# Value projection of the second layer by seven block products in place of eight

## The reference

```python
        else:
            o = layer // 2
            qc, kc, vc = jnp.split(h @ odd_w_in[o], 3, axis=-1)
            mix = stick_breaking_attention(qc, kc, vc) @ odd_w_out[o]
        h = layer_norm(DEEPNORM_ALPHA * h + mix, ln_mix_g[layer], ln_mix_b[layer])
        ffn = swiglu(h, ffn_w1[layer], ffn_w3[layer], ffn_w2[layer])
```

## Time and profile before

| | |
|---|---|
| median of 3 runs | 1157.35 us (1156.26 to 1157.83) |
| the profiled execution | 1156.23 us, its span 1154.5 us |
| PE busy | 1133.9 us, 98% of the span |
| PEld (weight loads of PE) | 988.1 us, 86% |
| DVE / ACT / POOL busy | 863.0 / 541.4 / 525.2 us |
| granted TensorE clock, mean | 0.998 of full speed |
| the chain that ended last | PE 92%, DVE 5%, ACT 1%, POOL 1% |

### The profile page before, as it was taken

One profiled execution on the slowest core, in us unless ns is written; L12 is line 12 of the kernel. 1 busy time (PEld: TensorE's weight loads), 2 busy tenths in 40 slices (PEclk: granted clock), 3 DMA queues, 4 the chain that ended last, 5 costly groups with the idle time before them and its releaser, 6 DMA issues.

```text
span 1154.5 us, 19191 instructions
## 1 busy us (share of the span) xinstructions
PE 1133.9 (98%) x7461; PEld 988.1 (86%) x7461; DVE 863.0 (75%) x1202; ACT 541.4 (47%) x849; POOL 525.2 (45%) x346
## 2 busy tenths in 40 slices
PE   7999999999999999999999999999999999999997
PEld 6877768899999999888887777777999999998886
DVE  8558652897888888994804787866987888879957
ACT  6335665245444544553335555532545454454540
POOL 6897614356567773010353232203576666760000
PEclk9999999999999999999999999999999999999999
DMA  7623315143333336234243111202433333352341
GB/s 213 186 76 93 109 65 201 39 126 110 110 100 103 108 105 192 72 113 143 86 133 91 56 56 55 67 8 74 130 89 111 110 105 97 100 179 88 96 123 73
DMA packets 160186, 121.00 MB, mean 105 GB/s; under 512 B 19376, under 2 KB 140248, under 8 KB 160096
## 3 DMA queue, kind: packets, MB, share of 16 engines
q1 hardware_dynamic: 160096, 119.77, 34.7%
HBM read 116.32 MB, written 3.43 MB: 104 GB/s over the span
## 4 chain that ended last, share of the span: by engine, by line
PE 92%; DVE 5%; ACT 1%; POOL 1%; issue 1%; SPq 0%; DMA 0%; DVEq 0%; ACTq 0%; POOLq 0%
PE ps L2122 18%; PE ps L2124 17%; PE ps L2123 17%; PE ps L2154 5%; PE ps L2152 5%; PE ps L2153 5%; PE ps L2145 5%; PE ps L2147 5%; PE ps L2146 5%; PE ps L2661 2%; PE ps L2687 2%; PE ps L2672 2%; PE ps L2159 1%; PE ps L2705 1%; PE ps L2384 1%; PE ps L2707 1%
## 5 line engine op out<-in xcount | busy, mean ns | idle before, releaser
L848 POOL TENSOR_TENSOR wlo<-raw,whi 128x1024 fp32r<-128x1024 f32 x75 | 183.2, 2454 | 333.4 <-ACT whi L973 326.4
L2122 PE MATMUL ps<-xhi,whi 128*128 128x256 f32 (+1 forms) x848 | 272.1, 321 | 0.0
L2124 PE MATMUL ps<-xhi,wlo 128*128 128x256 f32 (+1 forms) x848 | 267.0, 315 | 0.0
L2123 PE MATMUL ps<-xlo,whi 128*128 128x256 f32 (+1 forms) x848 | 266.9, 315 | 0.0
L2122 PEld LDWEIGHTS ps<-xhi,whi 128*128 128x128 f32 x848 | 161.7, 191 | 17.6 <-issue 6.4
L927 POOL TENSOR_TENSOR wlo<-raw,whi 128x512 fp32r<-128x512 f32 x114 | 173.2, 1546 | 0.6 <-ACT whi L1235 0.4
L2124 PE MATMUL ps<-thi,wlo 128*128 128x256 f32 x608 | 172.2, 283 | 0.0
L2123 PE MATMUL ps<-tlo,whi 128*128 128x256 f32 x608 | 172.2, 283 | 0.0
L2122 PE MATMUL ps<-thi,whi 128*128 128x256 f32 x608 | 172.2, 283 | 0.0
L2124 PEld LDWEIGHTS ps<-xhi,wlo 128*128 128x128 f32 x848 | 161.8, 191 | 10.4
L2123 PEld LDWEIGHTS ps<-xlo,whi 128*128 128x128 f32 x848 | 161.9, 191 | 8.5
(11 more groups left out here) (293 smaller groups left out, 2355.6 us busy)
## 6 DMA issues: line engine op xcount, KB each, us to landing
raw<-in_ffn_w SPq DMA_DIRECT2D x126, 512.0 KB, 3.9
raw<-in_odd_w_in SPq DMA_DIRECT2D x24, 512.0 KB, 3.7
raw<-in_even_w_in SPq DMA_DIRECT2D x16, 512.0 KB, 4.5
t<-in_ffn_w SPq DMA_DIRECT2D x12, 512.0 KB, 6.4
h<-in_x SPq DMA_DIRECT2D x8, 512.0 KB, 5.0
raw<-in_even_w_out SPq DMA_DIRECT2D x8, 512.0 KB, 3.8
raw<-in_odd_w_out SPq DMA_DIRECT2D x8, 512.0 KB, 3.5
bias<-rel_scratch SPq DMA_DIRECT2D x8, 256.0 KB, 3.5
```

Source lines behind the costliest of these rows:

```text
L848: eng.tensor_tensor(lo, raw_of(b), hi, ALU.subtract).then_inc(w_lo, 1)
L2122: eng.matmul(o_, w_hi_, x_hi_, start=start, stop=False)
L2123: eng.matmul(o_, w_hi_, x_lo_, start=False, stop=False)
L2124: return eng.matmul(o_, w_lo_, x_hi_, start=False, stop=stop)
```

## The change

The token rows, the k values and the columns are each cut in half, x = [[A11, A12], [A21, A22]] and W = [[B11, B12], [B21, B22]], and the four quarters of the result come from seven products of quarter matrices (256 tokens x 512 k x 512 columns), in Winograd's form of Strassen's scheme:

- P1 = A11·B11, P2 = A12·B21, P4 = A22·(B21 − B22 + B12 − B11), P7 = (A11 − A21)·(B22 − B12), P6 = (A21 + A22 − A11)·(B22 − B12 + B11), P5 = (A21 + A22)·(B12 − B11), P3 = (A12 + A11 − A21 − A22)·B22;
- C11 = P1 + P2, C12 = P1 + P6 + P5 + P3, C21 = P1 + P4 + P7 + P6, C22 = P1 + P7 + P6 + P5. In the code P6 is summed onto P7 in the same two banks, so C12 first has P7 subtracted.

Each product is two units of 12 matmuls (two tiles of k, two token tiles, three products): 14 units, 168 matmuls, in the order P1, P2, P4, P7, P6, P5, P3. The first four units go through `overlapped`, now with one part each.

What comes with it:

- Loads: six blocks of 512 KB for P1, P2 and P3, and four more of 512 KB (`load_right_columns`: B12 and B22) straight into `v1` and `v2`, issued by SP after the last load of the output product; eight were there before.
- POOL: eight differences of weights of 128x1024 (`v_sums`). The two for P7 stand ahead of the wait for the last block of the output product, the six others after the lowering of the first block of P1. Then it lowers 14 blocks in place of 8; for four products the block is a difference, not a landed one.
- ACT: keeps the unrounded x of the first two token tiles in `xf` (`keep_x`), copies P1 to `sg` (`keep_first`), rounds 14 blocks of weights and four sums of x (`s_upper`), and copies C11 to `ov`. The four copies of the whole result go.
- DVE: four sums of x (`s_sum` counts them), their four lowerings (`s_lower`), and 14 additions of 128x512 from PSUM (`v_add`).
- PE waits: P7 for the copy of C11 (`ov_out`), for its sum (`s_lowered`); P6, which adds onto P7 in the same banks, for the additions that read P7 (`v_added`); P3 likewise for those that read P5. The first of the products for queries and keys no longer waits for `ov_out`, the scores wait for all 14 additions.

```diff
-    for k in range(KT):
-        row_tiles(owi, k * P, 2 * D, D)
+    V_UNITS = [(p, part) for p in (P1, P2, P4, P7, P6, P5, P3) for part in range(2)]
+    V_END = OV + len(V_UNITS)
+    V_SUMS = [(P7, 0), (P7, 1), (P5, 0), (P6, 0), (P5, 1), (P6, 1), (P4, 0), (P4, 1)]
+    for p, part in V_UNITS:
+        if p in (P1, P2, P3):
+            k0 = 2 * part + (0 if p == P1 else KT // 2)
+            row_tiles(owi, k0 * P, 2 * D + S * (p == P3), S)
+        else:
+            load_of.append(None)
...
+        S_ORDER = (P7, P6, P5, P3)
+        V_BANK = {P1: 0, P2: 0, P4: 2, P7: 0, P6: 0, P5: 4, P3: 4}
+        V_FIRST = (P1, P7, P6, P5)
+        V_ADDS = ([(P4, 0), (P4, 1), (P7, 0), (P7, 1)] + [(P6, t) for t in range(2) for _ in range(3)]
+                  + [(P5, 0), (P5, 1), (P3, 0), (P3, 1)])
...
+                    if OV <= last < V_END and V_UNITS[last - OV][0] != P3:
+                        p, part = V_UNITS[last - OV]
+                        sp_.wait_ge(v_sum, v_sum_upto(P5 if p == P1 else P4, part))
...
+                    if b == out_end(0) - 1:
+                        load_right_columns()
...
+            def load_right_columns():
+                sp_.wait_ge(joint_lo, GS)
+                for part in range(2):
+                    for k0, p in ((0, P5), (KT // 2, P6)):
+                        eng.dma_start(v_store(p, part), tiles_of(owi, (k0 + 2 * part) * P, 2 * D + S, S, 2)).then_inc(
+                            right_landed[part], 16)
...
+            def v_sums(p, part):
...
+                if p == P7:
+                    pool.wait_ge(right_landed[part], 32)
+                    pool.wait_ge(w_used, ordinary(out_first(0) + max(
+                        u for u, unit in enumerate(UNITS[0]) if unit[0] == HALF1) + 1))
+                    o_, a, b_ = t3_, t2_, t1_
+                if p == P5:
+                    pool.wait_ge(*landed(v_block(P1, part)))
+                    pool.wait_ge(v_sum, v_sum_upto(P7, part))
+                    o_, a, b_ = t1_, t1_, upper
+                if p == P6:
+                    pool.wait_ge(v_sum, v_sum_upto(P5, part))
+                    o_, a, b_ = t2_, t2_, t1_
+                if p == P4:
+                    pool.wait_ge(*landed(v_block(P2, part)))
+                    pool.wait_ge(v_sum, v_sum_upto(P6, part))
+                    o_, a, b_ = t4_, lower, t2_
+                eng.tensor_tensor(o_, a, b_, ALU.subtract).then_inc(v_sum, 1)
+
+            v_sums(P7, 0)
+            v_sums(P7, 1)
             pool.wait_ge(w_lo, ordinary(out_end(0)))
-            norm(1, OV)
+            lower_upto(OV + 1)
+            for p, part in V_SUMS[2:]:
+                v_sums(p, part)
+            lower_upto(V_END)
             lower_upto(OQK + LEAD + 4)
...
+                    if summed(b):
+                        act.wait_ge(v_sum, v_sum_upto(*V_UNITS[b - OV]))
...
+                def keep_x(t):
+                    act.wait_ge(x_ready, NT * (n + 1) + t + 1)
+                    eng.copy(xf[:, :, t * P:(t + 1) * P],
+                             psf[:, 2 * t * S:2 * t * S + D].rearrange("p (k n) -> p k n", k=KT)).then_inc(xf_ready, 1)
+
                 for t in range(NT - 1):
                     if n < 3 and t == 2:
                         upper_x(n + 1, 0)
+                        if n == 1:
+                            keep_x(0)
                         upper_x(n + 1, 1)
                     std(t)
                 upper_upto(f + 3)
+                if n == 1:
+                    keep_x(1)
+                    keep_first(0)
                 std(NT - 1)
-                if n < 3:
+                if n == 1:
+                    keep_first(1)
+                    upper_x(2, 2)
+                    upper_upto(f + 4)
+                    upper_x(2, 3)
+                elif n < 3:
                     upper_upto(f + 4)
                     upper_x(n + 1, 2)
                     upper_x(n + 1, 3)
...
+            def keep_first(t):
+                if t == 0:
+                    act.wait_ge(v_first, 1)
+                else:
+                    act.wait_ge(w_used, v_used(P1))
+                eng.copy(sg[:, t, :], ps[:, V_BANK[P1] + t, :]).then_inc(v_kept, 1)
+
+            def s_upper(p):
+                act.wait_ge(s_sum, S_ORDER.index(p) + 1)
+                if p == P3:
+                    act.wait_ge(w_used, v_used(P7))
+                eng.copy(s_part(s_hi, p), s_full[:, S_ORDER.index(p) % 2]).then_inc(s_rounded, 1)
...
             ffn(0)
             upper_upto(OV)
             norm(1, OV)
-            for k in range(KT):
-                upper_upto(OV + k)
+            upper_upto(v_block(P7, 0))
+            s_upper(P7)
+            s_upper(P6)
+            upper_upto(v_block(P7, 1))
+            act.wait_ge(w_used, v_used(P2))
+            eng.copy(ov[:, 0:2, 0:S], ps[:, V_BANK[P2]:V_BANK[P2] + 2, :]).then_inc(ov_out, 1)
+            upper_upto(v_block(P6, 0))
+            s_upper(P5)
+            upper_upto(v_block(P5, 0))
+            s_upper(P3)
             upper_upto(OQK + 3)
-            for i, t in enumerate(OV_ORDER):
-                if i < NT - 1:
-                    act.wait_ge(ov_done, i + 1)
-                else:
-                    act.wait_ge(w_used, ordinary(OV + KT))
-                eng.copy(ov[:, t, :], psf[:, 2 * t * S:2 * (t + 1) * S]).then_inc(ov_out, 1)
...
+            def s_lower(p):
+                dve.wait_ge(s_rounded, S_ORDER.index(p) + 1)
+                tt(s_part(s_lo, p), s_full[:, S_ORDER.index(p) % 2], s_part(s_hi, p).bitcast(F32),
+                   ALU.subtract).then_inc(s_lowered, 1)
...
+            def v_add(o_, a, p, t, op=ALU.add):
+                if p in V_FIRST and t == 0:
+                    dve.wait_ge(v_first, V_FIRST.index(p) + 1)
+                else:
+                    dve.wait_ge(w_used, v_used(p))
+                tt(o_, a, ps[:, V_BANK[p] + t, :], op).then_inc(v_added, 1)
...
+            dve.wait_ge(xf_ready, 2)
+            tt(s_of(0), first_rows(0).rearrange("p k (t n) -> p k t n", t=2), rows_late(0), ALU.subtract).then_inc(s_sum, 1)
+            dve.wait_ge(s_sum, 1)
+            tt(s_of(1), rows_late(KT // 2), s_of(0), ALU.subtract).then_inc(s_sum, 1)
+            s_lower(P7)
+            s_lower(P6)
+            dve.wait_ge(s_sum, 2)
+            dve.wait_ge(s_lowered, 1)
+            tt(s_full[:, 0], s_full[:, 1], first_rows(0), ALU.add).then_inc(s_sum, 1)
+            dve.wait_ge(v_kept, 2)
+            for t in range(2):
+                v_add(v_of(2 + t, 0), sg[:, t, :], P4, t)
+            s_lower(P5)
+            dve.wait_ge(s_sum, 3)
+            dve.wait_ge(s_lowered, 2)
+            tt(s_full[:, 1], first_rows(KT // 2), s_full[:, 1], ALU.subtract).then_inc(s_sum, 1)
+            for t in range(2):
+                v_add(v_of(t, 1), sg[:, t, :], P7, t, ALU.subtract)
+            s_lower(P3)
+            for t in range(2):
+                own_adds(P7, t)
+                v_add(v_of(t, 1), v_of(t, 1), P6, t)
+                own_adds(P4, t)
+                v_add(v_of(2 + t, 0), v_of(2 + t, 0), P6, t)
+                v_add(v_of(2 + t, 1), sg[:, t, :], P6, t)
+            for t in range(2):
+                own_adds(P6, t)
+                v_add(v_of(2 + t, 1), v_of(2 + t, 1), P5, t)
+            for t in range(2):
+                v_add(v_of(t, 1), v_of(t, 1), P3, t)
 
...
+            def v_unit(p, part):
...
+                    b = v_block(p, part)
+                    pe.wait_ge(w_lo, ordinary(b + 1))
+                    if p == P1:
+                        pe.wait_ge(xf_ready, 1)
+                    if p == P4:
+                        pe.wait_ge(xf_ready, 2)
+                    if p == P5:
+                        pe.wait_ge(s_sum, 2)
+                    if p == P7:
+                        pe.wait_ge(ov_out, 1)
+                    if p in S_ORDER:
+                        pe.wait_ge(s_lowered, S_ORDER.index(p) + 1)
+                    for t in range(2):
+                        if p == P2:
+                            pe.wait_ge(v_kept, t + 1)
+                        if p in (P6, P3):
+                            pe.wait_ge(v_added, v_added_upto(P7 if p == P6 else P5, t))
+                        for r in range(2):
+                            k = 2 * part + r
+                            if p in S_ORDER:
+                                c = slice(t * P, (t + 1) * P)
+                                hi, lo = (s_part(x_, p)[:, k, c] for x_ in (s_hi, s_lo))
+                            else:
+                                row = t + (2 if p == P4 else 0)
+                                c = slice(row * P, (row + 1) * P)
+                                hi, lo = (x_[:, k + (0 if p == P1 else KT // 2), c] for x_ in (xhi, xlo))
+                            w = slice(r * S, (r + 1) * S)
+                            mm = three_wide(ps[:, V_BANK[p] + t, :], hi, lo, whi[:, slot(b), w], wlo[:, slot(b), w],
```

(63 more changed lines are left out.)

27 lines of the change are left out of this document (23 added, 4 removed).

## The result

| kernel | median, us | ratio to before | 95% interval | value projection, us | PE's waits in it, us |
|---|---|---|---|---|---|
| before | 1156.80 | | | 45.34 | none |
| changed | 1161.77 | 1.0046 | 1.0031 to 1.0062 | 49.41 | 7.17 |

A forecast was written before the change was run, and what follows sets the result against it. PE alone was taken to bound the value projection. −5.44 + 0.07 + 7.75 gave +2.4, by the starts +2.2, taken as +2.3; with +1.6 for the clock +3.9, so 1157.35 + 3.9 = 1161.3 us, range 1157.3 to 1165.0.

The forecast's parts named there:

- 24 matmuls fewer: PE in the value projection: 24 matmuls less at a pitch of 0.2267 us, −5.44 us.
- the edits put at nothing: POOL's weight differences, four more loads and ACT's copies in the norm: each forecast at cost 0.
- The differences on POOL: Eight weight differences on POOL, hidden in its idle time and DVE's layer norm additions: cost 0, 1.8 us to spare.
- The rival of late differences: P7's two differences start 3 us late, PE waits near 543.3: up to 2 us more, 1163.3 us; chance 0.08.
- the fear for the loads: Four more 512 KB loads might come late for P7's differences; cost 0, else taken by POOL's 3.7 us of room.
- The path to P6: From the last x tile to P6: DVE reads P7 late, so PE waits before P6, +7.75 us.
- The walk: Step-by-step times from x's last tile, DVE and POOL taking turns: first P7 addition ends 594.05, PE waits until 594.1.
- the rival in which DVE comes first: DVE gets the port before POOL at P7's lowering: wait some 6 us, sum +2.5, 1159.9 us; chance 0.15.
- No turns, so faster: Rival: POOL and DVE run side by side, P7 is read by 585.7, only −5.44 + 0.2 remains: 1152.1 us; chance 0.17.
- The clock, +1.6: After the wait before P6 PE restarts at the lower clock, 1.2 GHz: +1.6 us, between ends 0 and 5.4.
- The doubt about the clock column: Recorded clock might be unreliable, reading 1.00 beside slow transposes; by the column the sum is +2.3, by durations +3.9.
- The sum: All terms for the value projection, passed on whole to the run: +2.3 + 1.6 = +3.9 us.

The follow-up runs named there:

- after_again: The changed kernel measured once more, nothing altered: 1161.20 us, 1.0036 of before.
- e3_busy_wait: The changed kernel plus 56 transposes of the identity on PE into an unread bank, right ahead of P6: 1159.55 us, 1.0018 of before.
- e2_reads_first: The changed kernel with P7's two additions moved on DVE ahead of the lowering of P5's sum and the fourth sum: 1159.55 us, 1.0020 of before.
- e8_block_first: e2_reads_first with ACT's rounding of P5's second block moved ahead of that of P3's sum: 1159.44 us, 1.0015 of before.

## Why the prediction held, point by point

- **24 matmuls fewer: −5.44 us.** In the two kernels without any wait the stage is 39.90 against 45.34: −5.44. That also settles the edits put at nothing, as far as they reach the projection.
- **The differences on POOL, cost 0.** POOL, then DVE's last lowering of the output product and POOL's next block:

```profile
537.29 5.75 POOL L1024 TENSOR_TENSOR v<-v,v 128x1024 f32<-128x1024 f32 x2 [36.74 <-PE ps L2334]
...
556.82 4.76 POOL L1024 TENSOR_TENSOR v<-raw,v 128x1024 f32<-128x1024 f32 x2
565.34 4.78 POOL L911 TENSOR_TENSOR wlo<-raw,whi 128x1024 fp32r<-128x1024 f32 x2 [3.76 <-ACT whi L1066]
...
543.51 1.21 DVE L1559 TENSOR_TENSOR wlo<-raw,whi 128x1024 fp32r<-128x1024 f32 x1
```

  That lowering ends at 544.72, on the clock of before 541.56 against the forecast's 541.5; the six others end at 561.58, 3.76 us before POOL's next task. PE has no wait there. The rival of late differences falls, and so does the fear for the loads.
- **The path to P6.** The walk, each end shifted by 3.16 us, beside the trace: P6's sum lowered 587.4, read 587.36; s3 590.8, read 590.70; P4's additions 592.1, read 591.89; P5's sum 593.2, read 593.04; s4 596.6, read 596.31; P6 begins 597.3, read 597.06. The first DVE lowering asked 0.17 us after POOL had begun (580.70 and 580.53), where the walk had 0.14, so the rival in which DVE comes first did not occur. The term was 7.75; from 589.73, where P6 would have begun, to 597.06 it is 7.33. P7's block ended later than the walk had it by 0.2 us, the rest is 0.2 us too much in the chain. That rival's own price was off: from the end 592.9 that it names, the wait would be 6.6 us and the sum +1.2, not +0.9.
- **No turns, so faster.** It fell as a forecast and is what the remedies show: 1151.64 to 1152.80 in four kernels, where 1152.1 was worked out.
- **The clock, +1.6.** The ten matmuls from 597.06 to 601.32 take 4.26 us and would take 2.27: +1.99; in after_again it is +1.7 (eight from 593.87 to 597.39). Its removal in e3_busy_wait gave 1.63 to 1.94. The row that the term was taken from, 16 transposes at the start of the run, came near, but no run shows why a start of the run and a wait inside it should cost the same: that part is luck. The doubt about the clock column was not needed in this place: 0.50 stands beside matmuls 0.43 us apart, about half of full speed.
- **The sum.** −5.44 + 7.33 + 1.99 = +3.88 of the 4.07 by which the stage grew; 0.11 of the rest lies at P7's start, where 0.07 was forecast (its first matmul 0.03 us late, the next 0.08), and 0.08 us is not accounted for. In run medians it is +5.0 and, with the kernel again, +3.6. The forecast's +3.9 held, with its terms right to 0.4 us each. That the sum came nearer than the terms is luck: the path was 0.42 us too long and the clock's term 0.39 too small. (The chances for slower add up to 0.68, not 0.67.)

What came out otherwise lay in the experiments, not in the prediction: I expected the reordering on DVE to be worth 4 to 5.6 us, and then the block's place on ACT another 3 to 5. The step that failed there was to follow only the wait in hand. The turns stay, five DVE instructions lengthened in the changed kernel, five in e2_reads_first and six in e8_block_first, and three engines working in order pass them on.

## What to carry to other kernels

When a change moves work to DVE and POOL at the same time, list which DVE instructions have both inputs in SBUF and which POOL ones read it, and walk their turns up to the first reader on the critical engine; 1.2 us became 3.3 to 3.4 here, four times ahead of that reader. If one input can stay in PSUM the turns vanish, while the two reorderings tried here mostly handed the wait on. A gap of PE is to be priced with the slow matmuls behind it: 1.7 to 2.0 us behind 7.2 us here, and 1.5 to 1.6 us in the two kernels that split the wait. Filling the gap with idle transposes took that part back.

## What the runs showed that was not expected

- In e2_reads_first a wait of 2.74 us ahead of P6 left the clock at 1.00; a wait of 2.63 us ahead of P5's second block was followed by a fall, to 0.59 in 604 to 606, though PE had been back at work since 603.37 and was busy in all of that stretch. e8_block_first repeats it: no fall behind 2.77 us ahead of P6, one behind 2.35 us ahead of P3, with PE back since 604.70 and the first slow matmul after 605.9. So the clock can fall behind a short wait, after PE has restarted. What tells the two waits apart these runs don't show.
- Splitting the wait hardly cut the loss at the lower clock: eight matmuls lose 1.6 us in e2_reads_first and 1.5 in e8_block_first, where PE's waits are 5.6 and 5.7 us in all, against 1.7 to 2.0 behind the single wait of 7.2.
